# A decoder layer in split fp32: one-row conditioning vector, reordered transposes, weight remainders on GpSimd, shifted weight tiles

## The chip, the cores and the metric

One core of one Trainium2 chip runs the whole layer in one launch. The metric is device microseconds. The kernel before was timed three times: median 1067.24 us, lowest 1066.86, highest 1069.26.

## The reference, cut to what matters

The input x is 512 tokens by 1024 features, fp32. Three sub-layers follow each other; each normalises x (RMSNorm), scales and shifts it by values made from a conditioning vector c (1024 values), computes, and adds the result back to x times a gate.

```
c_act = silu(c);  mod = c_act @ w_ada + b_ada          # 9 x 1024 scales, shifts, gates
1: h = modulate(rms_norm(x));  x += 0.5 * gate * (silu(h @ Wg) * (h @ Wu)) @ Wout      # D_FF 2816
2: h = modulate(rms_norm(x));  split h @ w_in into u_pool, q_lat, kv_lat, k_rope, g_pool, g_mla
   br_pool = windowed means of u_pool, grouped product, projection
   q, k, v from rms_norm(q_lat), rms_norm(kv_lat);  8 heads of causal softmax attention -> br_mla
   x += gate * (sigmoid(g_pool) * br_pool + sigmoid(g_mla) * br_mla) @ w_out
3: as 1, with its own weights
```

## The kernel before, in words

**Arithmetic.** Every large product is made of three matmuls in a reduced fp32 format: each operand is split into a high part (a rounded copy) and a low part (operand minus high part), and `product` (lines 456 to 461) adds high*high, low*high and high*low. Weights arrive by DMA in slots of 128 x 2048 fp32 (`w_raw[0]`, `w_raw[1]`); ScalarE (ACT) writes the high part to `w_hi`, VectorE (DVE) subtracts to get `w_lo` (`split`, line 1340), and TensorE (PE) uses both. The same is done for the activations `h_hi`, `h_lo`. Order between the engines is written out by hand: five in-order queues (PE, ACT, DVE, GpSimd or POOL, and SP for all DMAs), joined by counting semaphores. Nothing is planned at run time, so what stands behind a waiting instruction on its queue waits as well.

**Start (`first_up`, `first_modulated`).** SP issues the constants, c copied to 128 rows (`c_wide`, 512 KB), four tiles of x, then 16 tiles of w_ada and three weight chunks in turn. ACT applies silu to `c_wide` (line 1286), loads its table for square roots and squares three x tiles; DVE makes the row scales. For each of 8 feature tiles k, DVE reduces one tile of w_ada for the scale and one for the shift, PE transposes x (`turned`, line 514), ACT writes `h_hi` and the full `scaled` copy, and DVE writes `h_lo` (`first_low`, line 1537). `part(c, k)` on PE waits for `h_lo` of tile k before any of its six matmuls.

**From FFN 1 to the mixer (`norm_mix`, `mixer`).** The last output tile of FFN 1 is done by column halves (`down_last`), so that the norm of tokens 0 to 255 (half 0) starts early. Half 0's norm runs on DVE as `scale_pair`, `low_pair` (pairs of tiles), with ACT's `high` between; the weight chunks LAT 0 and LAT 1 (2016 columns each) are split among them: ACT `mix_first(0)`, `mix_first(1)`, `mix_split(1)`, DVE the same three. PE runs half 0's latent products for k = 0..7, with `norm_sum(1, 1)` (sums of squares of half 1, needs ACT's `last_square(1, 1, ...)`) after k = 1 and `norm_wide(1, 1)` (spreads the scales of half 1, needs DVE's `norm_diag`) after k = 7. Later PE computes four pool groups, then turns the latents (line 728), then starts the KV products, which wait for all four pool groups to be copied out of PSUM (`u_evac` 4).

**Keys and heads.** PE turns 8 query heads, computes gate unit 0 (24 x 2 matmuls of 8 k), turns 8 key heads (line 790) and starts head 0. ACT takes `k_hi`, DVE `k_lo` (line 1777) per head; DVE then runs `gate(0)` (line 1770), and the row maxima, scales and splits of head 0. The probabilities are transposed by PE at line 840 once `p_scaled` counts four.

**Merge and output product.** For tile m of 8, DVE gates `tanh_mla` (line 1845), POOL adds `br_pool` (line 2038), ACT takes the high part, DVE the low part (line 1590). In the midst of it, at m = 4, ACT and DVE split the first chunk of w_out. The last chunk of w_out and the first two chunks of FFN 2 are done by column halves, beside the norm of sub-layer 3 (`norm_ffn2`, `up_by_halves`).

The lines that say where a wait stands:

```
def part(c, k):
    pe.wait_ge(h_ready, k + 1)
...
    pe.wait_ge(u_evac, 4)                      # ahead of the KV products
...
    pe.wait_ge(k_t_evac, 5)                    # ahead of head 0
```

Of the kernel before, what the change touches and what calls it, by code (L numbers as in the profile page):

```python
# [5 lines left out]
ALU = mybir.AluOpType  # L6
# [58 lines left out]
K_BANK = (1, 2, 3, 4, 0, 5, 6, 7)  # L65
# [11 lines left out]
def program(nc, x_t, x_rows, c_rows, w_ada, w_ffn_in, w_ffn_out, w_mix, mix_consts, positions, consts, out):  # L77
    ctx = ExitStack()
    with ctx:
# [22 lines left out]
        w_raw = [place(f"w_raw{i}", [P, SLOT]) for i in range(2)]  # L102
        w_hi = [place(f"w_hi{i}", [P, SLOT], F32R) for i in range(2)]
        w_lo = [place(f"w_lo{i}", [P, SLOT], F32R) for i in range(2)]
        const_sb = place("const_sb", [P, P + 72 + 3 * KD])
# [25 lines left out]
        c_wide = place("c_wide", [P, D], at=scaled_at + 4096)  # L131

# [8 lines left out]
        w0_lo = place("w0_lo", [P, SLOT], F32R, at=w0_at + 8 * SLOT)  # L141
        first_raw, first_w_hi, first_w_lo = (w0_raw, w_raw[1], w_raw[0]), (w0_hi, w_hi[1], w_hi[0]), (w0_lo, w_lo[1], w_lo[0])
# [68 lines left out]
        c_in = sem("c_in")  # L211
        x_in = [sem(f"x_in{t}") for t in range(TOK)]
# [14 lines left out]
        half_lo_done = sem("half_lo_done")  # L227
        rstd_ready = sem("rstd_ready")
# [109 lines left out]
        def _(sp):  # L338
# [116 lines left out]
        def _(pe):  # L455
# [7 lines left out]
            def w_tile(slot, t):  # L463
                cols = slice(t * P, (t + 1) * P)
                return w_hi[slot][:, cols], w_lo[slot][:, cols]

# [23 lines left out]
            def ffn(f):  # L490
# [26 lines left out]

                def part(c, k):
# [13 lines left out]
                def first_up():  # L532
# [3 lines left out]
                    part(0, 0)  # L536
# [38 lines left out]
                def up_half(s, hf, k):  # L575
                    hi, lo = ((w_hi[0], w_lo[0]), (w0_hi, w0_lo))[s]
# [6 lines left out]
                def up_by_halves():  # L583
# [3 lines left out]
                    for k in range(KD):  # L587
                        pe.wait_ge(half_ready[0], KD + k + 1)
                        up_half(0, 0, k)
                        if k == 2:  # L590
                            norm_sum(2, 1)
                        if k == 7:
                            norm_wide(2, 1)
                    pe.wait_ge(spare_lo, 1)
                    pe.wait_ge(gu_evac, NF + 2)
                    for k in range(KD):
                        up_half(1, 0, k)
# [15 lines left out]
                def down_last():  # L613

                    pe.wait_ge(out_evac, KD)
                    for hf in range(2):
                        for half in range(2):
                            pe.wait_ge(lo_done, n0 + NF + 14 + half + 1)
                            for k in range(NFH):
                                cols = half_cols(hf)  # L620
                                last = product(bank[5 + hf][:, cols], w_tile(half, k),
# [47 lines left out]
            def mixer():  # L669
# [11 lines left out]
                for k in range(KD):  # L681
                    if k < 3:
                        pe.wait_ge(half_lo_done, 2)
                    elif k < 6:
                        chunk(LAT_AT)
                    else:
                        chunk(LAT_AT + 1)
# [5 lines left out]
                    if k == 7:  # L693
# [1419 lines left out]
```

## Time and profile before

| what | value |
|---|---|
| median of 3 runs | 1067.24 us (1066.86 to 1069.26) |
| the profiled execution's own time, and its span | 1066.83 us, 1065.0 us |
| PE busy (matmul) | 1037.0 us, 97% |
| PE weight loads | 877.5 us, 82% |
| DVE, ACT, POOL busy | 537.1, 374.3, 62.0 us |
| DMA | 138.64 MB, mean 130 GB/s; 36% of the 16 engines |
| chain that ended last, share of PE | 93% |

PE's busy time counts overlapping matmuls once, and says little of its rate: what counts is from one start to the next. A 512-column matmul starts every 0.227 us in the long stages, a 256-column one every 0.12 us. The span is cut at the instructions; 1.83 us of the run's time lie around it. Times of rows are microseconds from the start of the span; "x2" on a row means two instructions merged.

### The profile page before, as it was taken

The numbers are of one execution on the slowest core, as the hardware profiler recorded it, in microseconds if no ns is written. First come the engines' busy times: TensorE is split into PE (matmuls) and PEld (weight loads), VectorE is DVE, ScalarE is ACT, GpSimd is POOL, SyncE is SP. The second block draws the span as 40 slices with busy tenths as digits, with TensorE's granted clock in tenths as the row PEclk, the third lists the DMA queues.
The fourth block names the chain that finished last, engine by engine and source line by source line (L and its number), as shares of the span: only waits on it lengthen the run. The fifth ranks groups of instructions, "written<-read, shape, count | busy, mean of one in ns | idle before, by whom it ended". The sixth has DMA issues, their size and how long they took to land.

```text
span 1065.0 us, 12725 instructions
## 1 busy us (share of the span) xinstructions
PE 1037.0 (97%) x4990; PEld 877.5 (82%) x4990; DVE 537.1 (50%) x754; ACT 374.3 (35%) x522; POOL 62.0 (6%) x56
## 2 busy tenths in 40 slices
PE   2999999999999999999999999999999999999998
PEld 2888888888888899898888887898888888888887
DVE  5765656555664265777675555564333333232221
ACT  6633232232321234577544533333323223221211
POOL 0000000000000000820100003200000000000000
PEclk9999999999999999999999999999999999999999
DMA  9765454545564332223121122213222222223222
GB/s 352 298 237 202 177 217 163 228 160 200 205 236 150 115 113 93 82 80 114 45 79 50 70 79 88 93 59 114 84 95 102 83 114 79 94 81 103 88 91 96
DMA packets 28879, 138.64 MB, mean 130 GB/s; under 512 B 3248, under 2 KB 3504, under 8 KB 21168
## 3 DMA queue, kind: packets, MB, share of 16 engines
q1 hardware_dynamic: 28848, 138.23, 35.8%
q8 instruction: 19, 0.31, 0.1%
q14 instruction: 12, 0.10, 0.0%
HBM read 136.12 MB, written 2.10 MB: 130 GB/s over the span
## 4 chain that ended last, share of the span: by engine, by line
PE 93%; DVE 2%; ACT 1%; DMA 1%; issue 1%; POOL 1%; SPq 1%; DVEq 0%; ACTq 0%; POOLq 0%
PE bank L459 31%; PE bank L461 30%; PE bank L460 30%; DMA ada_first<-w_ada 1%; PE bank L840 1%; POOL h L2038 1%; ACT w_hi L929 0%; PE bank L790 0%; DVE k_lo L1777 0%; DVE tanh_mla L1845 0%; PE bank L514 0%; ACT h_hi L958 0%; DVE h_lo L1417 0%; SPq L412 0%; PE bank L479 0%
## 5 line engine op out<-in xcount | busy, mean ns | idle before, releaser
L459 PE MATMUL bank<-h_hi,w_hi 128*128 128x512 f32 (+1 forms) x976 | 373.4, 383 | 5.1 <-DVE h_lo L1537 2.8
L461 PE MATMUL bank<-h_lo,w_hi 128*128 128x512 f32 (+1 forms) x976 | 370.8, 380 | 0.0
L460 PE MATMUL bank<-h_hi,w_lo 128*128 128x512 f32 (+1 forms) x976 | 370.8, 380 | 0.0
L1342 DVE TENSOR_TENSOR w_lo<-w_raw,w_hi 128x2048 fp32r<-128x2048 f32 (+3 forms) x93 | 189.8, 2041 | 147.5 <-ACT w_hi L929 147.5
L459 PEld LDWEIGHTS bank<-h_hi,w_hi 128*128 128x128 f32 x976 | 184.4, 189 | 40.6 <-DVE h_lo L1537 3.2
L461 PEld LDWEIGHTS bank<-h_lo,w_hi 128*128 128x128 f32 x976 | 184.2, 189 | 35.1
L460 PEld LDWEIGHTS bank<-h_hi,w_lo 128*128 128x128 f32 x976 | 184.5, 189 | 33.9
L929 ACT ACTIVATE w_hi<-w_raw 128x2048 fp32r<-128x2048 f32 (+3 forms) x93 | 158.7, 1707 | 121.2 <-PE bank L461 77.8
L459 PE MATMUL bank<-act_hi,w_hi 128*128 128x512 f32 (+1 forms) x374 | 141.1, 377 | 0.0
L460 PE MATMUL bank<-act_hi,w_lo 128*128 128x512 f32 (+1 forms) x374 | 140.8, 377 | 0.0
L461 PE MATMUL bank<-act_lo,w_hi 128*128 128x512 f32 (+1 forms) x374 | 140.8, 376 | 0.0
L1220 ACT ACTIVATE scaled<-bank 128x512 f32<-128x512 f32 x44 | 26.3, 597 | 275.0 <-PE bank L461 275.0
L1875 DVE TENSOR_TENSOR scaled<-scaled,bank 128x512 f32<-128x512 f32 x44 | 30.2, 687 | 166.1 <-ACT scaled L1220 166.0
L460 PEld LDWEIGHTS bank<-act_hi,w_lo 128*128 128x128 f32 x374 | 70.4, 188 | 13.0
L461 PEld LDWEIGHTS bank<-act_lo,w_hi 128*128 128x128 f32 x374 | 70.4, 188 | 13.0
L459 PEld LDWEIGHTS bank<-act_hi,w_hi 128*128 128x128 f32 x374 | 70.4, 188 | 12.7
L1347 DVE CUSTOM_DVE_ANT_0 ada_raw<-ada_raw,c_wide,const_sb 128x1024 f32<-128x1024 f32 x56 | 69.9, 1281 | 5.1 <-DMA ada_raw<-w_ada 5.0
L1879 DVE TENSOR_TENSOR act_lo<-scaled,act_hi 128x512 fp32r<-128x512 f32 (+1 forms) x44 | 30.5, 692 | 35.6 <-ACT act_hi L1224 35.6
L1943 DVE SCALAR_TENSOR_TENSOR x<-bank,out_gate,x 128x512 f32<-128x512 f32 (+1 forms) x15 | 11.3, 751 | 61.0 <-PE bank L461 61.0
L1224 ACT ACTIVATE act_hi<-scaled 128x512 f32 (+1 forms) x44 | 27.8, 632 | 39.1 <-DVE scaled L1875 39.1
L938 ACT ACTIVATE scaled<-x 128x512 f32<-128x512 f32 (+1 forms) x13 | 8.2, 630 | 60.1 <-DVE x L1943 43.2
L1810 DVE TENSOR_TENSOR p_lo<-bank,p_hi 128x512 fp32r<-128x512 f32 (+1 forms) x24 | 13.0, 596 | 22.6 <-ACT p_hi L1007 22.6
(196 smaller groups left out, 887.3 us busy)
## 6 DMA issues: line engine op xcount, KB each, us to landing
w_raw<-w_ffn_in SPq DMA_DIRECT2D x41, 1024.0 KB, 4.8
ada_raw<-w_ada SPq DMA_DIRECT2D x56, 512.0 KB, 5.2
w_raw<-w_ffn_out SPq DMA_DIRECT2D x32, 704.0 KB, 4.0
w_raw<-w_mix SPq DMA_DIRECT2D x19, 1024.0 KB, 4.8
ada_first<-w_ada SPq DMA_DIRECT2D x16, 512.0 KB, 12.7
w_raw<-w_ffn_in SPq DMA_DIRECT2D x6, 512.0 KB, 12.8
x_tok<-x_rows SPq DMA_DIRECT2D x4, 512.0 KB, 7.2
x<-x_t SPq DMA_DIRECT2D x4, 512.0 KB, 5.6
```

The costliest lines, as they stand in the source:

```text
L459: nc.tensor.matmul(dst, a_hi, b_hi, start=start, stop=False)
L460: nc.tensor.matmul(dst, a_lo, b_hi, start=False, stop=False)
L461: return nc.tensor.matmul(dst, a_hi, b_lo, start=False, stop=stop)
L929: nc.scalar.activation(w_hi[slot][:, 0:size], w_raw[slot][:, 0:size], ACT.Copy).then_inc(hi_done, 1)
L1220: nc.scalar.activation(silu_g, bank[banks[0]][:, :], ACT.Silu).then_inc(silu_done, 1)
L1224: nc.scalar.activation(act_hi[f][:, bass.ds(j, 1), :], prod, ACT.Copy).then_inc(act_hi_done, 1)
L1342: nc.vector.tensor_tensor(w_lo[slot][:, 0:size], w_raw[slot][:, 0:size], w_hi[slot][:, 0:size].bitcast(F32), ALU.subtract).then_inc(lo_don ...
L1347: nc.vector.tensor_tensor_reduce(out=raw, in0=raw, in1=c_wide[:, :], scale=1.0, scalar=bias_ada[:, col:col + 1], op0=ALU.mult, op1=ALU.add ...
L1810: nc.vector.tensor_tensor(p_lo[:, at:at + n, :].rearrange("p b q -> p (b q)"), bank[b][:, 0:n * P], p_hi[:, at:at + n, :].bitcast(F32).rea ...
L1875: nc.vector.tensor_tensor(prod, silu_g, bank[banks[1]][:, :], ALU.mult).then_inc(gu_evac, 1)
L1879: nc.vector.tensor_tensor(act_lo[f][:, bass.ds(j, 1), :], prod.unsqueeze(1), act_hi[f][:, bass.ds(j, 1), :].bitcast(F32), ALU.subtract)\
L1943: nc.vector.scalar_tensor_tensor(out=xm, in0=bank[4 + s // 2][:, :].unsqueeze(1), scalar=out_gate[:, bass.ds(m, 1)], in1=xm, op0=ALU.mult, ...
```

## The change

1. **c as one row.** c is loaded as 1 x 1024 ahead of the constants; PE spreads it over 128 rows by two fp32 matmuls with a row of ones, ACT applies silu in two halves out of PSUM. `part_high_first(0, 0)`: the first part does its four matmuls with `h_hi` as soon as `h_hi` is there. DVE's `first_low(0)` goes ahead of `scale_tile(1)`.
2. **Norm of the mixer, remainders on GpSimd.** The low parts of LAT 0 and LAT 1 are made by POOL in four pieces of 1008 columns; ACT's high parts are in four pieces, in another order; `norm_wide(1, 1)` stands after k = 4 instead of 7, `norm_var` and `norm_diag` ahead of the last `low_pair`.
3. **Latents** are turned ahead of the last pool group.
4. **Keys.** Gate unit 0 is cut in two; four key heads are turned ahead of its second half, four after it, with new banks; head 0 waits for 4 key heads instead of 5. The low part of gate chunk 1 (2048 columns) is made by POOL; ACT's split and `gate(0)` stand after four key heads.
5. **Merge.** ACT splits the chunk of w_out at m = 2, DVE after the gating of m = 3. `gain_cols(2)` is moved out of `norm_ffn2` to ahead of the merge.
6. **Norm of FFN 2.** The first two chunks are computed together for k = 0..3, with `norm_sum` after k = 0 and `norm_wide` after k = 3; `norm_var`, `norm_diag` and ACT's `norm_std` stand earlier.
7. **64 bytes.** The split weights used by 256-column products of the last output tiles and of FFN 2's first two chunks lie 64 bytes further (`late_hi`, `late_lo`, `spare_w_hi`, `spare_w_lo`).

```diff
-K_BANK = (1, 2, 3, 4, 0, 5, 6, 7)
+K_BANK = (1, 2, 3, 0, 5, 6, 7, 4)
...
+            sp.dma_start(c_row[:, :], c_rows).then_inc(c_in, 16)
             sp.dma_start(const_sb[:, :], consts).then_inc(const_in, 16)
-            sp.dma_start(c_wide[:, :], c_rows).then_inc(c_in, 16)
...
+                def part_high_first(c, k):
+                    pe.wait_ge(first_h, 2 * k + 1)
+                    pe.wait_ge(first_lo[c], k + 1)
...                                            # hi*hi and lo*hi of both gu
+                    pe.wait_ge(h_ready, k + 1)
...                                            # hi*lo of both gu
                     else:
-                        chunk(LAT_AT + 1)
+                        pe.wait_ge(second_lo_done, 1)
...
-                    if k == 7:
+                    if k == 4:
                         norm_wide(1, 1)
+                chunk(LAT_AT + 1)
...
                     for g in range(2):
+                        if c and g:
+                            lat_turned()
...
-                unit(0, slot)
+                unit(0, slot, 0, 4)
                 pe.wait_ge(qk_tok_ready, 2)
                 for h in range(HEADS):
+                    if h == 4:
+                        unit(0, slot, 4, KD)
...
-                pe.wait_ge(k_t_evac, 5)
+                pe.wait_ge(k_t_evac, 4)
...
             def norm_mix():                    # ACT
                 last_square(1, 0, 7, 1)
                 norm_std(1, 0)
                 mix_first(0)
+                high(1, 0, 0)
+                high(1, 0, 1)
                 mix_first(1)
+                high(1, 0, 2)
+                high(1, 0, 3)
+                mix_second(0)
+                last_square(1, 1, 7, KD + 2)
+                high(1, 0, 4)
+                high(1, 0, 5)
+                norm_std(1, 1)
+                mix_second(1)
...
                 query_high(0)
-                mix_split(GATE_AT + 1)
-                gate(0)
                 for h in range(HEADS):
+                    if h == 4:
+                        mix_split(GATE_AT + 1)
+                        gate(0)
...
                 for m in range(KD):            # ACT, merge
-                    if m == 4:
+                    if m == 2:
                         mix_split(WOUT_AT)
...
                 for m in range(KD):            # DVE, merge
-                    if m == 4:
-                        mix_split(WOUT_AT)
...
+                    if m == 3:
+                        mix_split(WOUT_AT)
...
+            def chunk_low(k, cols):            # POOL
+                slot = (MIX_CHUNK + k) % 2
+                pool.wait_ge(hi_done, MIX_CHUNK + k + 1)
+                return nc.gpsimd.tensor_tensor(w_lo[slot][:, cols], w_raw[slot][:, cols], w_hi[slot][:, cols].bitcast(F32),
+                                               ALU.subtract)
...
             pool.wait_ge(qk_t_ready, 2 * HEADS)
...                                            # mask_wide, two small instructions
+            chunk_low(GATE_AT + 1, slice(0, SLOT)).then_inc(lo_done, 1)
```

## Rows read from the trace of the kernel before

**Rows 1.** What PE waited for: us in total, times, longest.
```profile
PE bank L459 <- DVE h_lo L1537: 2.8, 1, 2.8
PE bank L459 <- DVE h_lo L1590: 1.9, 1, 1.9
PE bank L459 <- DVE k_lo L1777: 1.5, 1, 1.5
PE bank L479 <- ACT sq_last L949: 0.8, 1, 0.8
```

**Rows 2.** Timeline of the start: start, us, engine, line, operation, tiles.
```profile
8.93 1.06 ACT L1291 ACTIVATE square_note<-x_tok 128x1024 f32<-128x1024 f32 x1 [1.04 <-DMA x_tok<-x_rows]
17.93 0.78 ACT L1210 ACTIVATE h_hi<-bank,mod,gain_mod 128x512 fp32r<-128x512 f32 x1
...
20.48 0.69 DVE L1537 TENSOR_TENSOR h_lo<-scaled,h_hi 128x512 fp32r<-128x512 f32 x1
```

**Rows 3.** DMA issues: KB each, median us from issue to landing.
```profile
const_sb<-consts SPq DMA_DIRECT2D x1, 112.0 KB, 2.1
```

**Rows 4.** Timeline around an fp32 matmul of 256 columns (L487), PE.
```profile
382.29 0.59 PE L487 MATMUL bank<-diag,ones_r 128*128 128x256 f32 x2
382.53 0.47 PE L459 MATMUL bank<-act_hi,w_hi 128*128 128x256 f32 x1
382.83 0.28 PE L460 MATMUL bank<-act_hi,w_lo 128*128 128x256 f32 x1
```

**Rows 5.** Timeline of the mixer's norm, DVE.
```profile
383.71 1.20 DVE L1432 TENSOR_TENSOR w_lo<-w_raw,w_hi 128x1008 fp32r<-128x1008 f32 x1
385.03 0.89 DVE L1417 SCALAR_TENSOR_TENSOR h_lo<-scaled,mod,h_hi 128x256 fp32r<-128x256 f32 x2
```

**Rows 6.** Timeline, POOL: a 16-column and a 512-column subtraction or addition.
```profile
448.01 0.22 POOL L2017 TENSOR_TENSOR window<-window,mixc 128x16 f32<-128x16 f32 x1
...
341.69 1.30 POOL L1986 TENSOR_TENSOR ssq<-ssq,scaled 128x512 f32<-128x512 f32 x1 [13.60 <-ACT scaled L938]
```

**Rows 7.** Timeline, DVE beside POOL, two places.
```profile
640.60 1.30 POOL L2038 TENSOR_TENSOR h<-tanh_mla,br_pool 128x512 f32<-128x512 f32 x1
641.33 1.12 DVE L1590 TENSOR_TENSOR h_lo<-h,h_hi 128x512 fp32r<-128x512 f32 x1 [1.27 <-ACT h_hi L1007]
...
445.54 1.49 DVE L1342 TENSOR_TENSOR w_lo<-w_raw,w_hi 128x1152 fp32r<-128x1152 f32 x1
445.89 2.04 POOL L2014 TENSOR_TENSOR window<-window 128x512 f32<-128x512 f32 x1
446.95 1.12 DVE L1590 TENSOR_TENSOR lat<-lat,mixc 128x128 f32<-128x128 f32 x1
```

**Rows 8.** Timeline of the latents' end, ACT and PE.
```profile
440.97 0.60 ACT L1007 ACTIVATE u_pad<-bank 128x512 f32<-128x512 f32 x1 [4.84 <-PE bank L461]
...
443.73 0.47 PE L459 MATMUL bank<-w_hi,lat_hi 128*128 128x512 f32 x1 [0.62 <-DVE lat_lo L1663]
```

**Rows 9.** Timeline of head 0's start, DVE and PE.
```profile
507.49 0.68 DVE L1770 SCALAR_TENSOR_TENSOR br_pool<-scaled,br_pool 128x512 f32<-128x512 f32 x1
...
511.05 1.27 DVE L1803 TENSOR_SCALAR p_tok<-p_tok,row_inv 128x128 f32<-128x128 f32 x4
...
513.42 1.25 PE L840 MATMUL bank<-const_sb,p_tok 128*128 128x128 f32 x10
```

**Rows 10.** Timeline after the merge, PE; and its window (third last column: granted clock).
```profile
655.12 0.50 PE L459 MATMUL bank<-h_hi,w_hi 128*128 128x512 f32 x1 [1.87 <-DVE h_lo L1590]
656.55 0.63 PE L460 MATMUL bank<-h_hi,w_lo 128*128 128x512 f32 x1
656.98 0.63 PE L461 MATMUL bank<-h_lo,w_hi 128*128 128x512 f32 x1
...
655.12:662.00 6.88, 6.88 (x23) 5.36 (x24) 3.65 (x3) 3.83 (x5) 0.00 (x0) 0.75 0.04 6
```

**Rows 11.** Timeline of the last norm, DVE.
```profile
689.17 1.26 DVE L1401 SCALAR_TENSOR_TENSOR gain_mod<-mod,const_sb 128x8 f32<-128x8 f32 x1
```

More of the change, by code:

```diff
@@ L516, in turned @@
                     last.then_inc(x_turned, 1)
+                def part_high_first(c, k):
+                    cols = [slice((gu * KD + k) * P, (gu * KD + k + 1) * P) for gu in range(2)]
+                    pe.wait_ge(first_h, 2 * k + 1)
+                    pe.wait_ge(first_lo[c], k + 1)
+                    for gu in range(2):
+                        dst = bank[first_banks[c][gu]][:, :]
+                        nc.tensor.matmul(dst, first_w_hi[c][:, cols[gu]], h_hi[:, k, :], start=True, stop=False)
+                        nc.tensor.matmul(dst, first_w_lo[c][:, cols[gu]], h_hi[:, k, :], start=False, stop=False)
+                    pe.wait_ge(h_ready, k + 1)
+                    for gu in range(2):
+                        nc.tensor.matmul(bank[first_banks[c][gu]][:, :], first_w_hi[c][:, cols[gu]], h_lo[:, k, :],
+                                         start=False, stop=False)
                 def part(c, k):
@@ L620, in down_last @@
                                 cols = half_cols(hf)
-                                last = product(bank[5 + hf][:, cols], w_tile(half, k),
+                                last = product(bank[5 + hf][:, cols], late_tile(half, k),
                                                (act_hi[0][:, half * NFH + k, cols], act_lo[0][:, half * NFH + k, cols]),
@@ L913, in mixer @@
                             last.then_inc(tail_done, 1)
+            pe.wait_ge(c_in, 16)
+            pe.wait_ge(one_row_ready, 1)
+            for half in range(2):
+                nc.tensor.matmul(bank[half][:, :], one_row[:, :], c_row[:, S * half:S * half + S], start=True, stop=True)\
+                    .then_inc(c_spread, 1)
             pe.wait_ge(const_in, 16)
@@ L967, in mix_first, with mix_second @@
                     .then_inc(hi_done if part else half_hi_done, 1)
+            def mix_second(part):
+                act.wait_ge(raw_in[1], 16 * ((MIX_CHUNK + 1) // 2 + 1 - RAW_LATER[1]))
+                act.wait_ge(pe_used, FFN_CHUNKS)
+                n = MIX_SIZES[1] // 2
+                nc.scalar.activation(w_hi[1][:, n * part:n * part + n], w_raw[1][:, n * part:n * part + n], ACT.Copy)\
+                    .then_inc(hi_done if part else second_hi_done, 1)
             def norm_mix():
@@ L1266, in down @@
                         if not (last and s == 3):
-                            split((n0 + NF + s + 1) // 2 + 2 * i, (s + 1) % 2, OUT_ELEMS, (pe_used, u0 + q), f)
+                            split((n0 + NF + s + 1) // 2 + 2 * i, (s + 1) % 2, OUT_ELEMS, (pe_used, u0 + q), f,
+                                  late_hi if f == 0 and last and s else w_hi)
                         elif after:
@@ L1282, in ffn @@
                 down(3, True)
-            act.wait_ge(c_in, 16)
-            nc.scalar.activation(c_wide[:, :], c_wide[:, :], ACT.Silu).then_inc(c_ready, 1)
+            for half in range(2):
+                act.wait_ge(c_spread, half + 1)
+                nc.scalar.activation(c_wide[:, S * half:S * half + S], bank[half][:, :], ACT.Silu).then_inc(c_ready, 1)
             act.wait_ge(const_in, 16)
@@ L1929, in down @@
                         if not (last and s == 3):
-                            split(n0 + q + 1, (s + 1) % 2, OUT_ELEMS)
+                            late = f == 0 and last and s
+                            split(n0 + q + 1, (s + 1) % 2, OUT_ELEMS, late_hi if late else w_hi, late_lo if late else w_lo)
                         elif after:
```

152 lines of the change are left out of this document (87 added, 65 removed).

## Prediction

> **What bounds the kernel now.** I read the waits of TensorE (PE) first, then the timeline around each of them. PE is busy 97% of the span, so only its stops and its rate count. The reader is to see in [rows 1] how small the stops are: outside the start, 2.8 us before the first product of FFN 1, 1.9 us in the output product, 1.5 us ahead of head 0, 0.8 us in the mixer's norm; there are four more of 0.3 to 0.6 us. In the timelines one looks for the last event before each stop. At the start it is `h_lo` of tile 0 [rows 2]: `h_hi` is complete at 17.93 + 0.78 = 18.71, `h_lo` ends at 21.17, PE begins at 21.23. In the output product it is the low part of merged tile 6, and the stop costs more than 1.9 us: after it the matmuls start 0.43 us apart (656.55, 656.98) where 0.227 is the pace, and the window's granted clock is 0.75 [rows 10]: TensorE ran part of it at 1.2 GHz. Everything else on DVE, ACT and the queues has slack as long as it does not reach one of these places.
>
> I walked each stage through its queues in order, with the durations of the rows. The walk of the old order gives 396.1 for the second `norm_wide` (trace 396.3) and 655.2 for the product after the stop (trace 655.12), so the same walk of the new order is worth something. All sums are made against the profiled execution, 1066.83 us, which lies 0.4 us under the median.
>
> **A, the start.** `c_wide` (512 KB) leaves the queue, so x lands up to 1.3 us sooner. ACT does not gain all of it. The row of c lands about 2.1 us after its issue at 0.73, as `const_sb` did [rows 3]: 2.85. The price of the spreading: an fp32 matmul of 256 columns moves PE's next start by 382.83 - 382.29 - 0.12 = 0.42 us [rows 4], four passes over the columns at 2.4 GHz. So 512 columns at 1.2 GHz take 4 x 512 / 1.2 = 1.71 us, and two of them end at 6.3; silu's second half 7.0; the table of 1.3 us and a warm-up 8.5. The squares that began at 8.93 [rows 2] begin at 8.5, and -0.45 us is what reaches the row scales. PE then need not wait for `h_lo`: it starts at 18.71 - 0.45 + what ACT's order costs, about 18.8 instead of 21.2, does four products at the slow pace, and finds `h_lo` of tile 0 made (19.5 to 20.2, one w_ada reduction of 1.2 us sooner). Then the cover is gone: the next tiles' `h_lo` become the bound, since DVE's row of reductions is only 0.1 to 0.5 us ahead, and PE waits 0.24 us for tile 1 and 0.4 us for tile 2. The walk ends `first_up` 2.0 us sooner. Bounds: 1.5 (the row of c lands 0.5 later) and 2.8 (the spreading at full clock). **A = -2.0.**
>
> **B, the mixer's norm.** Before, DVE made the low parts of LAT 0 and 1 in 1.12 + 1.12 + 2.17 us; now POOL does, in four pieces of 1008 columns. Its price is not in the trace; from 0.22 us for 16 columns and 1.30 for 512 [rows 6] it is 0.22 + 992 x 2.18 ns = 2.38 us (bounds: 2.05, by the additions of 1.04 us, and 2.56, by proportion from 1.30), against 1.20 on DVE [rows 5]. What decides is that the two engines do not run side by side. At 641.33 DVE's `h_lo` of 512 columns took 1.12 us instead of 0.69 [rows 2], and ended 0.55 us after POOL's addition of 640.60 to 641.90 [rows 7]: it stood still until 0.13 us before POOL's end. At 445.89 it was POOL that stood still behind DVE's `w_lo`, and when that ended POOL went first, though DVE's next was issued too: that one took 1.12 us for 128 columns. All DVE instructions that waited this way read two SBUF operands. `low` (L1417) does, and so do the small steps of `norm_diag`. So each `low` can wait for a whole piece of 2.38 us. The walk: the first piece 383.6 to 386.0; PE starts k = 0 on time at 386.67; `low` of tile 0 at 385.85, then POOL's second piece 386.25 to 388.6 holds `low` of tile 1, so k = 1 starts at 389.0 instead of 387.6; tile 2 and all of ACT behind its `high(1, 0, 2)`, `mix_second(0)` and the square follow, and `norm_sum` starts at 391.8 (before: 389.5); the third piece (391.3) holds `low` of tile 4, the fourth (395.9 to 398.2) holds `norm_diag`, and `norm_wide` runs at 398.8 with k = 5, 6, 7 still to do. Half 1 begins at 405.7; before, at 400.2. **B = +5.45**, bounds +3.5 (2.05 us, pieces of 1.9 even) and +6.1. If POOL and DVE did not hold each other, it would be -1.1: the 0.8 us wait of [rows 1] goes, since the square is done when PE asks, and the rest is overlap.
>
> A rule speaks to just this. The Trainium skill, "SBUF — State Buffer", "Who interferes with whom", says that a VectorE instruction with two SBUF inputs and a GpSimd instruction that reads SBUF take the same read port, and that the one that came second waits out the other. The trace agrees, 1.12 us against 0.69. It gives B = +5.45 where a plain count of freed DVE time would give -1.1. The same skill, "GPSIMD Engine Reference", "Performance versus the Vector engine", has 4497 ns for a fp32 addition of 2048 columns on GpSimd; my line through the rows gives 4.65; with the page's figure B and D would be 0.3 us smaller.
>
> **C, latents.** The transposes (2.1 us) move ahead of the last pool group. The stop at 443.73 [rows 8] was for the low part of the latents; that one is made beside the group now. But `u_evac` 4 stands in the same place: the copy of the last group began 0.2 us after PE's end and took 0.6 (440.97 [rows 8]). It is late next: the stop of 0.9 us from start to start comes back as 0.8. **C = 0**, bounds -0.1 and +0.2.
>
> **D, keys and head 0.** Four key heads are turned before the second half of the unit, so their `k_lo` (0.66 each) is made beside it: PE can start head 0 at 504.0 instead of 505.94. ACT, behind its split and `gate(0)`, has `k_hi` 7 at 505.6, DVE its `k_lo` at 506.35. But POOL begins the subtraction of 2048 columns, 0.22 + 2032 x 2.18 ns = 4.65 us, after the mask, at 504.8, and holds the port until 509.3. DVE's `gate(0)` reads `scaled` and `br_pool`, both in SBUF, and stands still from 506.35 to 509.3; behind it on DVE stand the row maxima and `p_scaled`. Before, `gate(0)` at 507.49 led to the last `p_scaled` at 511.05 + 1.27 = 512.32, so 4.83 us later [rows 9]; now 509.3 + 4.83 = 514.15. PE's transposes, at 513.42 before without a wait, start at 514.2, and PE has stood 2.8 us. **D = +0.8**, bounds -1.9 (nothing held; the 1.5 of [rows 1] gone) and +1.2.
>
> **E, merge and output product.** With the split at m = 2 ACT does it (1.9 us) in its pause for POOL, and DVE's subtraction lies after tile 3 instead of 644.41. The walk has `merged_low` 6 at 652.9 instead of 655.1 and `merged_low` 7 at 653.8: PE wants them at 653.1 and 653.8, and stops 0.1 us. That is 2.1 us of stop, and with it goes the slow stretch: from 655.96 to 659.4 eight starts came 0.43 apart or nearly, 1.6 us lost [rows 10]. **E = -3.7**, bounds -2.0 (the slow stretch comes anyway) and -3.8. `gain_cols(2)` has 24 us of room where it now is.
>
> **F, the last norm.** `gain_cols(2)` took 1.26 us on the path, since it too stood behind POOL (689.17 [rows 11]). Without it the half outputs start with PE's end, 0.5 us sooner, and `norm_sum` waits 0.3 instead of 0.8; the second stop (0.6 us) keeps 0.35, as the sum now stands after k = 0 and ACT's square is late there. **F = -0.75**, bounds -0.3 and -1.2.
>
> **G, 64 bytes.** 420 matmuls of 256 columns are touched, at 0.12 us from start to start; the columns alone are 0.107. Ends: -5.6 us (all 13 ns gone) and +4.2 (10 ns more, the spread of the 336-column tiles, whose offsets alternate by 64 bytes: 0.148 to 0.164). Their mean is the same for both offsets, so I take **0**.
>
> **Sum.** -2.0 + 5.45 + 0 + 0.8 - 3.7 - 0.75 + 0 = -0.2. A stop of 1.9 us was followed by the slow clock at 655, one of 1.5 us at 505.94 was not [rows 1, 10]. B now stops PE 1.4, 1.8 and 3.3 us within 11 us: I add the price of one slow stretch, +1.6, for it, and none for D, whose stop stands alone. +1.4 on 1066.83 is **1068.2 us**; this case's own range is 1065 to 1071.
>
> **The rivals.** *1: the port doesn't bind.* If pieces of 1008 columns let DVE in between, or DVE goes first, B = -1.1 and D = -1.9: -2.0 - 1.1 - 1.9 - 3.7 - 0.75 = -9.4, 1057.4 us. For it: 1008 columns aren't in the trace, and DVE loses 4.4 us of work in a tight place. Against: [rows 7] and all other meetings of the two. *2, slower: D's stop drops the clock as well.* Place: PE after 514.2; price 1.6 us [rows 10]; it decides if 2.8 us of standing is enough, where 1.9 us was. 1069.8 us. For it: the length; against: PE worked without a pause before it. *3: the 64 bytes pay.* 7 ns of 13 over 420 matmuls, -2.9: 1065.3 us. For it: the 336-column tiles do react to offsets; against: their mean.
>
> **How the numbers follow.** What can be told from no change is 0.2%, 2.1 us: 1065.1 to 1069.4. Chances: forecast 0.50 (faster 0.08, same 0.30, slower 0.12), rival 1 0.27 (faster), rival 2 0.15 (same 0.03, slower 0.12), rival 3 0.08 (faster 0.05, same 0.03). Together faster 0.40, same 0.36, slower 0.24. The range of 8 in 10 reaches from the middle of rival 1, 1056.5, to the upper bounds of B with a slow stretch, 1071.5.
>
> **What would show it.** A: first product near 18.8, `first_up` over 2 us sooner. B: `h_lo` (L1417's successor) at up to 2.4 us while POOL subtracts, POOL pieces near 2.4 us, stops of PE between 387 and 399 (in old times). D: `gate(0)` of near 3.6 us on DVE and a stop of 2.8 us before the transposes of head 0. E: no stop over 0.3 us in the output product and granted clock 1.00 there. G: 0.12 us between 256-column starts. Wrong it would be if `low` kept its 0.48 us beside POOL, or if the 256-column pace moved.

## The result, and the profile after

The changed kernel takes 1082.25 us (median of 4 runs, 1080.15 to 1083.08) against 1067.15 us (1066.86 to 1069.26): ratio 1.0135, 95% interval [1.0122, 1.0149]. It is slower by 15 us, where I had 1068.2 and a range up to 1071.5. The profiled execution took 1081.75 us, with a span of 1079.9. Of all the runs reported below one, of the kernel of experiment 9, took 3796.43 us and counts in no ratio.

The page of the kernel after, its span and the head of its first part:

```profile
span 1079.9 us, 12740 instructions
...
PE 1058.1 (98%) x4994; PEld 886.1 (82%) x4994; DVE 541.1 (50%) x751; ACT 374.8 (35%) x524; POOL 78.9 (7%) x61
```

PE is even busier than before, so its rate is the place to look. Two windows of 100 us in the long stages, FFN 1 and FFN 2; columns: window, length, busy time (instructions) of PE, weight loads, DVE, ACT, POOL, then granted clock, DMA share, GB/s. The kernel before:

```profile
200.00:300.00 100.00, 100.00 (x442) 82.78 (x442) 56.97 (x69) 28.26 (x29) 1.91 (x2) 1.00 0.55 197
740.00:840.00 100.00, 100.00 (x443) 82.78 (x442) 34.57 (x28) 27.32 (x27) 0.00 (x0) 1.00 0.26 94
```

The kernel after:

```profile
200.00:300.00 100.00, 100.00 (x434) 81.96 (x433) 55.15 (x67) 28.15 (x29) 1.71 (x2) 1.00 0.56 197
740.00:840.00 100.00, 100.00 (x435) 81.90 (x434) 33.06 (x27) 27.33 (x27) 0.00 (x0) 1.00 0.27 95
```

No stop in either, the granted clock is 1.00 in both, and yet 8 matmuls fewer in 100 us. No edit of the change reorders the work of these loops. The timeline of PE shows which matmuls are late (start, duration), first before, then after:

```profile
200.50 0.39 PE L459 MATMUL bank<-h_hi,w_hi 128*128 128x512 f32 x1
200.73 0.39 PE L460 MATMUL bank<-h_hi,w_lo 128*128 128x512 f32 x1
200.95 0.39 PE L461 MATMUL bank<-h_lo,w_hi 128*128 128x512 f32 x1
201.18 0.39 PE L459 MATMUL bank<-h_hi,w_hi 128*128 128x512 f32 x1
```

```profile
200.67 0.40 PE L471 MATMUL bank<-h_hi,w_hi 128*128 128x512 f32 x1
200.90 0.40 PE L472 MATMUL bank<-h_hi,w_lo 128*128 128x512 f32 x1
201.14 0.39 PE L473 MATMUL bank<-h_lo,w_hi 128*128 128x512 f32 x1
201.36 0.40 PE L471 MATMUL bank<-h_hi,w_hi 128*128 128x512 f32 x1
```

Before, three products take 0.68 us from start to start; after, 0.69. Over 240 triples between 100 and 350 us the means of the three are 232.5, 234.1 and 226.7 ns after; before they were 226.6, 226.4 and 227.0 ns. The slow ones are the starts on either side of the product with the low weights; from the third product to the next first one nothing changed. Outside the stops and after 50 us, 3,767 matmuls of 512 columns start 231.15 ns apart on average; before it was 226.87. That is 3,767 x 4.28 = **16.1 us**, more than the whole loss. The 411 matmuls of 256 columns went the other way, from 119.86 to 113.98 ns, -2.4 us. After, in the last norm:

```profile
723.04 0.28 PE L472 MATMUL bank<-h_hi,late_lo 128*128 128x256 f32 x1
723.16 0.28 PE L473 MATMUL bank<-h_lo,late_hi 128*128 128x256 f32 x1
723.27 0.28 PE L471 MATMUL bank<-h_hi,late_hi 128*128 128x256 f32 x1
```

The rest looks as the walk had it. What PE waited for in the kernel after (us in total, times, longest); it answers to [rows 1]:

```profile
PE bank L882 <- DVE p_tok L1856: 2.6, 1, 2.6
...
PE bank L495 <- ACT sq_last L996: 2.0, 2, 1.6
PE bank L471 <- DVE h_lo L1480: 1.3, 1, 1.3
PE bank L471 <- issue: 0.7, 1, 0.7
```

The 1.9 us of the output product and the 1.5 us ahead of head 0 are gone. New are 2.6 us for `p_tok` of head 0 and two or three stops in the mixer's norm. The start, which answers to [rows 2]:

```profile
16.80 0.78 ACT L1271 ACTIVATE h_hi<-bank,mod,gain_mod 128x512 fp32r<-128x512 f32 x1
...
17.62 0.79 PE L541 MATMUL bank<-h_hi,w_hi 128*128 128x512 f32 x1 [0.57 <-ACT h_hi L1271]
...
18.27 0.69 DVE L1587 TENSOR_TENSOR h_lo<-scaled,h_hi 128x512 fp32r<-128x512 f32 x1 [1.56 <-ACT scaled L1271]
```

PE starts 0.6 us before `h_lo` is begun, as the split of the first part allows. In the mixer's norm, POOL's pieces and DVE's small steps, which answer to [rows 5, 7]:

```profile
386.68 2.38 POOL L2065 TENSOR_TENSOR w_lo<-w_raw,w_hi 128x1008 fp32r<-128x1008 f32 x1 [8.91 <-ACT w_hi L1013]
389.01 2.53 POOL L2059 TENSOR_TENSOR w_lo<-w_raw,w_hi 128x1008 fp32r<-128x1008 f32 x1
...
387.10 4.72 DVE L1480 SCALAR_TENSOR_TENSOR h_lo<-scaled,mod,h_hi 128x256 fp32r<-128x256 f32 x2 [0.30 <-ACT h_hi L1005]
...
398.52 2.32 DVE L1429 SCALAR_TENSOR_TENSOR rstd<-newton,rstd 128x2 f32<-128x2 f32 x1
```

Two `low` of 0.48 us each take 4.72 us together, and a step of two columns takes 2.32: each stood until a piece of POOL was done. The same at the keys, which answers to [rows 9], with the granted clock behind it (third last column of the window):

```profile
514.35 4.61 POOL L2059 TENSOR_TENSOR w_lo<-w_raw,w_hi 128x2048 fp32r<-128x2048 f32 x1
...
515.81 3.70 DVE L1824 SCALAR_TENSOR_TENSOR br_pool<-scaled,br_pool 128x512 f32<-128x512 f32 x1
...
523.72 1.99 PE L882 MATMUL bank<-const_sb,p_tok 128*128 128x128 f32 x10 [2.58 <-DVE p_tok L1856]
...
525.94 0.63 PE L472 MATMUL bank<-h_hi,w_lo 128*128 128x512 f32 x1
526.36 0.63 PE L473 MATMUL bank<-h_lo,w_hi 128*128 128x512 f32 x1
...
523.70:528.00 4.30, 4.28 (x17) 3.76 (x18) 2.61 (x5) 3.27 (x5) 0.00 (x0) 0.60 0.01 2
```

And at the latents, ACT's last pool copy and the KV products behind it, answering to [rows 8]:

```profile
451.36 0.60 ACT L1067 ACTIVATE u_pad<-bank 128x512 f32<-128x512 f32 x1 [4.24 <-PE bank L473]
...
452.06 0.47 PE L471 MATMUL bank<-w_hi,lat_hi 128*128 128x512 f32 x1 [0.73 <-issue]
```

### The profile page after: what moved, and what is told of

It is laid out like the page before. It is cut to its first block, busy times and chain, and to the rows that moved or that the text cites. A ratio compares the mean times of both kernels' runs of the same rounds, so it can differ in the third digit from the quotient of the medians.

```text
span 1079.9 us, 12740 instructions
## 1 busy us (share of the span) xinstructions
PE 1058.1 (98%) x4994; PEld 886.1 (82%) x4994; DVE 541.1 (50%) x751; ACT 374.8 (35%) x524; POOL 78.9 (7%) x61
## 4 chain that ended last, share of the span: by engine, by line
PE 95%; DVE 1%; ACT 1%; DMA 1%; issue 0%; SPq 0%; DVEq 0%; ACTq 0%
PE bank L471 31%; PE bank L472 31%; PE bank L473 30%; DMA w_raw<-w_ffn_in 1%; PE bank L882 1%; DVE h_lo L1480 0%; PE bank L829 0%; DVE br_pool L1824 0%; PE bank L495 0%; PE bank L530 0%; ACT k_hi L1193 0%; DVE k_lo L1830 0%; ACT h_hi L1005 0%; ACT p_tok L1201 0%; PE bank L756 0%
## 5 line engine op out<-in xcount | busy, mean ns | idle before, releaser
L471 PE MATMUL bank<-h_hi,w_hi 128*128 128x512 f32 x878 | 350.4, 399 | 0.0
L472 PE MATMUL bank<-h_hi,w_lo 128*128 128x512 f32 x878 | 349.4, 398 | 0.0
L473 PE MATMUL bank<-h_lo,w_hi 128*128 128x512 f32 x878 | 342.8, 390 | 0.0
L473 PEld LDWEIGHTS bank<-h_lo,w_hi 128*128 128x128 f32 x878 | 169.2, 193 | 38.6
L471 PEld LDWEIGHTS bank<-h_hi,w_hi 128*128 128x128 f32 x878 | 165.5, 188 | 36.9
L472 PEld LDWEIGHTS bank<-h_hi,w_lo 128*128 128x128 f32 x878 | 165.6, 189 | 33.8
L472 PE MATMUL bank<-act_hi,w_lo 128*128 128x512 f32 x330 | 131.1, 397 | 0.0
L471 PE MATMUL bank<-act_hi,w_hi 128*128 128x512 f32 x330 | 130.9, 397 | 0.0
L473 PE MATMUL bank<-act_lo,w_hi 128*128 128x512 f32 x330 | 128.6, 390 | 0.0
L1201 ACT ACTIVATE p_tok<-bank,row_max 128x128 f32<-128x128 f32 (+3 forms) x32 | 16.9, 528 | 23.1 <-DVE row_max L1846 22.4
```

The lines of the kernel that those rows point to most:

```text
L471: nc.tensor.matmul(dst, a_hi, b_hi, start=start, stop=False)
L472: nc.tensor.matmul(dst, a_lo, b_hi, start=False, stop=False)
L473: return nc.tensor.matmul(dst, a_hi, b_lo, start=False, stop=stop)
L1201: nc.scalar.activation(p_tok[:, at:at + qt + 1, :].rearrange("p b q -> p (b q)"), bank[qt][:, 0:(qt + 1) * P], ACT.Exp, bias=row_max[:, qt ...
```

## The experiments

The theory after this reading: the loss is the address of the low weights. Edit 7 needs room for the shifted tiles, and makes it with 128 bytes between `w_hi` and `w_lo` and 128 more behind `w_lo`. Before, `w_hi`, `w_lo`, `h_hi`, `h_lo` and `act_hi` all begin 128 bytes past a multiple of 512, and tiles are 512 bytes apart. After, the low weights begin 256 past one, and all that lies behind them, `act_hi` too, 384 past one. So counted modulo 256 bytes the low weights alone have left the common place. Two buffers are said to be in phase when they begin at the same place modulo 256. The rival: the new order of work puts other traffic beside the matmuls.

**1. Only the gaps.** The kernel before, and

```diff
+        cursor[0] += 128
         w_lo = [place(f"w_lo{i}", [P, SLOT], F32R) for i in range(2)]
+        cursor[0] += 128
```

> The kernel before with one edit: 128 bytes of free space between w_hi and w_lo, and 128 more behind w_lo. Nothing is reordered and nothing lies at +64. Theory 1 (addresses): the low weights lie 128 bytes off the phase of the high weights, and that alone makes the 512-column pitch 0.231 instead of 0.227 (0.2325, 0.234, 0.2267 for the three products). 3,775 such matmuls after 50 us by 4.3 ns, and 100 before: 1067.2 + 16.6 = 1083.8 us. Rival 2 (the order of the work): the pitch rose because the new order leaves other traffic beside the matmuls; then this kernel is at 1067.2 us and 0.227.

Measured 1081.75 us against 1066.66, ratio 1.0137 [1.0121, 1.0154]; 231.14 ns between 3,786 starts. Its long stages:

```profile
200.00:300.00 100.00, 100.00 (x435) 81.84 (x434) 55.81 (x70) 26.35 (x27) 0.61 (x1) 1.00 0.56 198
740.00:840.00 100.00, 100.00 (x435) 81.84 (x434) 33.05 (x27) 27.32 (x27) 0.00 (x0) 1.00 0.26 95
```

435 matmuls in 100 us, as in the changed kernel, with not one instruction moved. The rival is out: two free gaps of 128 bytes cost 15 us. The pitch alone would make it 16.2 (3,786 x 4.27 ns); about 1.6 of that is hidden because this execution has no stretch at 1.2 GHz behind the stop of the output product (granted clock 1.00 between 655 and 670), which the one of before has [rows 10]. The second gap moves everything behind the low weights by 256 bytes as well; experiment 3, in which only the tiles move, and experiment 9 show that this is not what costs.

**2. The change without edit 7.** The changed kernel; both gaps removed, and

```diff
-        late_hi = [... at=cursor[0] + 4 * SLOT * i + 64) ...]     # late_lo, spare_w_hi, spare_w_lo alike
+        late_hi = [... at=cursor[0] + 4 * SLOT * i) ...]
```

> The changed kernel without its seventh edit: no gaps, and the tiles of the 256-column products at their old addresses. Theory 1: pitches 0.227 and 0.120 again, 1082.2 - 16.6 + 2.6 = 1068.2 us; it also is the sum that I had forecast for edits 1 to 6. Rival 2: it stays near 1082 us, pitch 0.231.

Measured 1067.86 us (11 runs) against 1066.66 (15 runs): 1.0005 [0.9995, 1.0014], pitches (from one start to the next) 226.89 ns at 512 columns and 119.86 at 256. Edits 1 to 6 together change nothing that can be told. As the pitch is that of before, its trace can be laid beside the one of before stage by stage; this is used below.

**3 and 4. Which offsets.** Weights of FFN 2's down projection at offsets of their own for each chunk, products of 512 columns in one kernel, of 2 x 256 in the other:

```diff
+OFFS = [(high, low), ...]
-    last = product(bank[4 + mm][:, :], w_tile(half, k), ...)
+    oh, ol = OFFS[2 * m + half]
+    tile = (w_hi[half][:, oh + k * P:oh + k * P + P], w_lo[half][:, ol + k * P:ol + k * P + P])
```

> The kernel before; in the 16 chunks of FFN 2's down projection each chunk's high and low weights are written and read at byte offsets of their own (loops unrolled for it): (high, low) = (0,0) (64,64) (0,128) (64,192) (128,128) (192,192) (256,256) (32,32) (384,384) (0,64) (64,0) (0,256) (0,32) (448,448) (96,96) (0,512). 33 matmuls of 512 columns each. Theory 1a, only the difference high to low counts: 0.2267 for all equal pairs and (0,512), 0.231 for the others. Theory 1b, the place itself counts (all tiles start 128 bytes past a multiple of 512 in the kernel before): equal pairs differ from each other; (64,64) at 0.220, by the 7 ns that the 256-column products gained. Rival 2: 0.227 everywhere.

> As the map of 512 columns, but each product of FFN 2's down projection is done in two column halves of 256, each in its own PSUM bank, with the same 16 pairs of offsets; twice the matmuls, so some 1067 + 7 us. Theory 1a: 0.120 for equal pairs, and (64,192) no better than (0,128). Theory 1b: (0,0) 0.120, (64,64) and (64,192) 0.113 as in the changed kernel; the rest shows which offset pays.

Mean ns from start to start, 33 matmuls (512 columns) and 66 (256) for each pair, added to the place of before:

```
high, low   0,0   0,256 0,512 256,256  0,128 128,128 64,192 0,64  64,0  64,64 192,192 448,448 384,384 0,32  32,32 96,96
512 cols   226.6 227.0 226.8 227.3    231.5 232.5   231.9  231.1 233.0 233.4 229.1   229.2   232.0   233.2 233.0 234.2
256 cols   119.9 120.0 119.8 120.0    119.3 118.6   113.7  117.7 117.8 117.8 117.8   117.7   120.0   118.4 118.3 118.7
```

The border from the pair (0,0) to (64,64) in the timeline of the first of the two: starts 0.22 to 0.23 apart up to 949.29, 0.23 to 0.24 behind it.

```profile
948.84 0.39 PE L462 MATMUL bank<-act_hi,w_lo 128*128 128x512 f32 x1
949.07 0.39 PE L463 MATMUL bank<-act_lo,w_hi 128*128 128x512 f32 x1
949.29 0.40 PE L461 MATMUL bank<-act_hi,w_hi 128*128 128x512 f32 x1
949.53 0.39 PE L462 MATMUL bank<-act_hi,w_lo 128*128 128x512 f32 x1
949.76 0.40 PE L463 MATMUL bank<-act_lo,w_hi 128*128 128x512 f32 x1
```

Each of the two kernels ran once (1069.06 and 1072.47 us). Theory 1a falls: in (64,64) and (128,128) high and low weights are in phase with each other and still cost 6 to 7 ns. 1b holds as to the place, but its number does not: no pair brings 512 columns under 226.6. Pairs that are alike modulo 256 agree within 0.7 ns, with one exception: (128,128) and (384,384) at 256 columns, 118.6 and 120.0. The kernel before has the best place for 512 columns and one of the worst for 256, and the two want different ones. That the pair (0,256) is as good as (0,0) is the way out for a layout that needs room.

**5 and 6. Place against what.** (Run once each, 1072.97 and 1072.66 us.) Tiles 576 bytes apart in FFN 2's down projection, so that each chunk walks through all phases; then the same with the moving operands 64 bytes further:

```diff
+    # ACT and DVE write, PE reads: tile k at k * (P + 16) elements; low weights 16 * m elements further
 act_hi = [place(f"act_hi{f}", [P, NF, S], F32R, at=act_at) ...]        # second kernel: at=act_at + 64, act_lo alike
```

> The kernel before; in FFN 2's down projection the weight tiles lie 576 bytes apart instead of 512, so that tile k of a chunk begins 64 k bytes further than before (mod 512), and the low weights of output tile m begin 64 m bytes further still. In the first chunk of each m the matmuls have 512 columns, in the second they are done in halves of 256. This scans all 8 x 8 pairs of phases in steps of 64 bytes. If only the phase modulo 256 counts: 0.227 for 512 columns where both phases are 0 or 256, 0.229 to 0.235 elsewhere; for 256 columns 0.120 there, 0.118 elsewhere and 0.1135 where high and low are 128 apart and neither is at 0 or 128 (the map had 0.1137 at (64,192)). If the phase modulo 512 counts, (320,320) differs from (64,64), as the changed kernel's spare tiles suggest: there both halves lie at 320 and the pitch was 0.113.

> The same scan with the moving operands act_hi and act_lo 64 bytes further. Theory P, the place of the weights alone counts: the same table. Theory Q, the place of the weights against that of the moving operand counts: the whole table is shifted by one step along the diagonal, and (64,64) has the 0.227.

The row of both tables in which the low weights lie 64 bytes past the high ones, mean ns of the three products of 512 columns for tiles k = 0 to 10 (place of the high weights 64 k):

```
moving at 0:    233.7 232.7 230.0 232.3 227.3 230.0 237.0 232.3 227.0 230.3 236.7
moving at +64:  229.3 228.3 230.0 237.0 232.3 227.3 230.3 236.7 232.3 227.3 229.7
```

From k = 4 on the second row is the first shifted by one tile: what counts is where the weights lie against the moving operand, theory Q. Over all eight rows, k = 5 to 9, the second kernel's tiles differ from the first's by 0.5 ns on average when shifted by one tile and by 2.8 when not, and those of 256 columns by 0.1 and 1.6. The shift fails in one kind of row, at 512 columns where high and low weights are in phase with each other; there it misses by up to 2.7 ns. The pattern comes back after four tiles, 256 bytes, from k = 3 on in the row shown (its first three do not fit it), and rows whose low weights differ by 256 bytes agree within 0.7 ns from k = 1 on. Not all of the expectation came: two tiles in phase with the moving operand take 230.7 to 231.0 in the first kernel and 230.3 to 232.7 in the second, never 227 but for the very first tile (226.7), and the (64,192) of 256 columns is not at 113.5 but at 118 here. In these kernels a tile's neighbours lie elsewhere too; that this makes the difference is likely and not shown, so the tables with constant offsets are the ones to use.

**7 and 8. Edits 2 and 4 undone; edit 2's order with DVE.** Both without edit 7; the second keeps the new order of the norm and puts the four remainders back on DVE (`mix_low`, between the pairs):

```diff
                 scale_pair(1, 0, 0)
+                mix_low(0, 0, half_hi_done, 2, half_lo_done)
                 low_pair(1, 0, 0)
+                mix_low(0, 1, hi_done, MIX_CHUNK + 1, lo_done)
                 scale_pair(1, 0, 2)
```

> The changed kernel without edits 2, 4 and 7: mixer norm and keys as before, the start, the latents, the merge and the last norm as changed. Theory (the stages add up as the trace of the kernel without edit 7 shows them): -2.15 start, +0.1 latents, -3.7 merge, -0.5 last norm: 1066.7 - 6.2 = 1060.5 us. Rival: the merge was only in time because the stops before it had let DVE and ACT run ahead; then the output product stops again and it is 1063 to 1064 us.

> As the one without edits 2, 4 and 7, but with edit 2's new order of the mixer norm, its four remainders of 1008 columns made by DVE instead of GpSimd. Theory (the shared port costs, not the order): no stop over 0.8 us between 384 and 400, and 0.5 to 1.5 us faster than the kernel without edit 2: 1059.3 us. Rival (the new order itself costs the 4.9 us of the mixer norm): 1065.3 us.

Measured 1060.27 us, ratio 0.9921 [0.9901, 0.9941], and 1061.85, 0.9938 [0.9916, 0.9959]; the kernel before had its median at 1069.14 in the runs beside these (7, from 1066.34 to 1070.21), against 1066.66 and 1067.21 beside the other experiments, so these two ratios flatter by some 0.2%. The first is the sum of the stages to 0.2 us. The second did not bring its 1.2 us, nor did the new order cost 4.9: in its trace the stage of the norm costs 1.4 us more than in the first's, and most of that is a stretch at 1.2 GHz behind a stop of 1.4 us. Its window:

```profile
384.00:400.00 16.00, 14.93 (x89) 14.63 (x88) 14.58 (x37) 8.61 (x18) 0.37 (x3) 0.89 0.36 123
```

(1.00 in the same window of the first.) So at least 3.4 of the 4.9 us are the GpSimd remainders', and the new order without them gains nothing. The port shows directly: with no piece of POOL beside it, the step of two columns that took 2.32 us takes 0.16, and two `low` take 0.87 us instead of 4.72.

The first's trace has such a stretch elsewhere. The keys are untouched in it, and yet behind the same stop of 1.5 us:

```profile
505.60 0.63 PE L469 MATMUL bank<-h_hi,w_hi 128*128 128x512 f32 x1
506.03 0.63 PE L470 MATMUL bank<-h_hi,w_lo 128*128 128x512 f32 x1
506.46 0.63 PE L471 MATMUL bank<-h_lo,w_hi 128*128 128x512 f32 x1
...
503.00:512.00 9.00, 8.45 (x34) 7.04 (x35) 6.38 (x20) 3.43 (x11) 3.48 (x4) 0.81 0.10 41
```

while the kernel before, at the same place, has

```profile
505.90:515.00 9.10, 9.06 (x49) 7.85 (x50) 6.14 (x20) 4.31 (x13) 2.97 (x4) 1.00 0.04 16
```

The same code after the same stop ran at 1.2 GHz for a while in one execution and not in the other: 1.6 us. The profiled execution of the first kernel took 1061.85 us, its other three, at a mean granted clock of 1.000 instead of 0.998, 1060.05 to 1060.33.

**9. The change with its layout mended.** The changed kernel, with

```diff
-        cursor[0] += 128
-        late_lo = [... at=cursor[0] + 4 * SLOT * i + 64) ...]
+        cursor[0] += 256
+        late_lo = [... at=cursor[0] + 4 * SLOT * i + 192) ...]
```

and 256 bytes behind `w_lo` instead of 128.

> The changed kernel with one edit: the two gaps are 256 bytes instead of 128, and the shifted low weights lie at +192 instead of +64. So w_lo is back in phase with w_hi and with the moving operands, while the 256-column products keep the pair (64,192), which the map had at 0.1137. Theory (relative place modulo 256 bytes): 512 columns 0.2267, 256 columns 0.1135, all else as changed: 1082.2 - 16.6 = 1065.5 us. Rival (any gap costs, or 256 is not the period in all slots): 1069 to 1082 us.

Measured 1066.01 us, 0.9983 [0.9971, 0.9995] against before (1067.21, 17 runs); 226.89 and 113.73 ns, and 443 matmuls in the window again:

```profile
200.00:300.00 100.00, 100.00 (x443) 82.82 (x442) 58.30 (x71) 27.11 (x28) 1.91 (x2) 1.00 0.56 191
```

Its three numbers, 256, 192 and 256, are worth 16.2 us. In this trace the shifted tiles bring 0.7 us in FFN 1's last output tile and 1.5 us in the last norm over the kernel without edit 7.

**10 and 11. The versions that the runs point to.** Edits 1, 3, 5, 6 and the mended 7; then also edit 4's order, with the remainder of the gate chunk on DVE:

```diff
                 query_low(0)
-                mix_split(GATE_AT + 1)
                 for h in range(HEADS):
+                    if h == 4:
+                        mix_split(GATE_AT + 1)
                     dve.wait_ge(k_hi_done, h + 1)
```

> Edits 1, 3, 5 and 6 with the mended layout; the mixer norm and the keys as before (no remainders on GpSimd). 1060.3 - 2.6 = 1057.7 us. If the 256-column pitch was hidden behind waits in the halves (the norm bound, not PE), under 1.5 us is gained and it is above 1058.8 us.

> As the last, with edit 4's order of keys and gate unit 0, but the remainder of gate chunk 1 made by DVE after the fourth key head, not by GpSimd. Theory (the port, not the order, cost the 2.8 us of that stage): head 0 starts 1.7 us sooner, PE then meets p_scaled at about 512.3 in old times and keeps 1.1 us: 1056.6 us. Rival (DVE is late by its own work there): at 1057.7 us or above.

Measured 1059.57 us, 0.9928 [0.9914, 0.9943], and 1057.45 us, 0.9911 [0.9897, 0.9925]. The first's six runs lie at 1058.1 to 1058.2 (two) and 1059.4 to 1060.3 (four), and the median is over my bound of 1058.8; the profiled one is of the lower group, at 1058.13, and in its trace the 256-column stages bring 2.1 us over those of the kernel without them. A slow stretch of 1.6 us, as above, would make the two groups, and the mean granted clock agrees: 1.000 in both runs of the lower group and 0.998 in all four of the upper one. No trace of the upper group was taken, so where it lies is open. Of the second's six runs four lie at 1057.3 to 1057.5 (clock 1.000) and two at 1058.7 and 1059.1 (0.998). In its trace head 0 starts 1.67 us sooner, and 0.7 of that is kept when PE asks for `p_scaled`; I had expected 1.1 and 1056.6 us:

```profile
PE bank L881 <- DVE p_tok L1863: 0.8, 1, 0.8
```

The intervals of the two overlap, but runs of the same granted clock do not: at 1.000 the second takes 1057.29 to 1057.49 us and the first 1058.13 and 1058.19, 0.75 more, as the traces say. So the order of edit 4 gains 0.7 us, and what it cost in the changed kernel came with the GpSimd remainder.

**12. The pair (64,64) instead of (64,192).**

```diff
-        late_lo = [... at=cursor[0] + 4 * SLOT * i + 192) ...]
+        late_lo = [... at=cursor[0] + 4 * SLOT * i + 64) ...]
```

> As the kernel with the keys' remainder on DVE, but the shifted low weights lie at +64, not +192, so high and low are in phase: pair (64,64). The map of 256 columns had 0.1178 there and 0.1137 at (64,192); in the map each tile is used for both halves in turn, here once. In the changed kernel the spare tiles had (64,64) too, and 0.113. If the map carries over: 308 matmuls of the shifted slots at 0.1178, +1.3 us, 1058.7 us. If the spare tiles carry over, the pair (64,64) is as good: 0.113 and 1057.4 us, and the gap of 128 bytes was never needed for the 256-column products.

Measured 1058.86 us, 0.991 [0.9893, 0.9928] (before: 1067.05). The 316 matmuls of the shifted slots are at 116.0 ns, between the 117.8 of the map and the 113.9 of (64,192); the 95 of the spare tiles at 114.2. So the 128 bytes between high and low do pay for 256 columns, about 0.7 us in all. The rest of the 1.4 us is not the pair's: this trace begins FFN 1 at 18.60, that of experiment 11 at 17.82. Why the spare tiles, also at (64,64), do not need the 128 bytes is open; modulo 512 they are at (64,64) and the shifted ones at (64,320).

## Why the prediction was wrong

**G, 64 bytes: the step that failed.** I took it at 0, between -5.6 and +4.2, for "420 matmuls of 256 columns are touched". Measured: -2.4 us on these (rival 3's mechanism, at 5.9 of 13 ns instead of 7), and +16.1 us on 3,767 matmuls of 512 columns that I had not counted at all. With the +1.5 of edits 1 to 6 below, 1066.83 + 1.5 - 2.4 + 16.1 = 1082.0, and the profiled execution took 1081.75. The error is in the question "what does the edit touch". The diff line `cursor[0] += 128` moves every buffer placed behind it, `w_lo` among them, which one of three products reads and the one before it stands next to. I had the hint in my own text: "the 336-column tiles, whose offsets alternate by 64 bytes: 0.148 to 0.164" suggests that a place changes a matmul's pace. I used it for the 420 that the edit names, and not for the 3,800 that it moves.

The Trainium skill, "TensorE: Matmul & The Clock Gate", "Step-by-step: what each phase is for", says that loading the next tile's weights takes no read bandwidth from the running matmul. By that one would not expect the place of the weights to matter. Here the mean pace changes from 226.6 ns to 229 to 234 with nothing but the place of the weights against the moving operand, and the measurement decides; whether the load or something else makes it, no run shows.

**Edits 1 to 6.** I had -0.2 + 1.6 = +1.4 us on 1066.83. The trace of the kernel without edit 7 has +1.5 at its last matmul, and the comparison 1.0005 [0.9995, 1.0014]. By stages, from the starts of the first matmuls behind each (us, before and without edit 7):

```
                                   before   without 7   stage    forecast
first product of FFN 1              21.23    18.23                 18.8
FFN 1 down                         265.10   262.95     -2.15   A  -2.0
pool groups begin (behind B)       418.97   421.70     +4.88   B  +5.45, and +1.6 clock
KV products                        443.73   446.58     +0.12   C   0
head 1's scores                    521.84   527.50     +2.81   D  +0.8 (rival 2: +2.4)
output product, its 256 columns    685.54   687.52     -3.68   E  -3.7
FFN 2 down                         941.76   943.22     -0.52   F  -0.75
```

**A** and **E** are right in place and size. In A the first product came earlier than the walk had it (18.23 for 18.8), and the tiles behind it gave 0.85 us back instead of 0.4. In E the stop and the slow stretch went together, as I had it; with the stretch 1.6 of the 3.7. **C** is right: PE stands 0.73 us. The view gives no releaser ("issue"), but the last pool copy ended at 451.96 in the kernel after and PE began at 452.06, so it is `u_evac` 4.

**B** has the mechanism: POOL's pieces take 2.32 to 2.53 us (forecast 2.38), `low` and `norm_diag`'s steps stand behind them. The first two stops came at 1.5 and 1.9 from start to start (forecast 1.4 and 1.8), and the fourth piece and `norm_wide` within 0.5 us of the walk (396.19, which is 398.34 in old times; forecast 398.8). The slow stretch came too (granted clock 0.91 between 384 and 402), but it lay before the third stop and was swallowed by it: between 391.5 and 394.6 twelve starts are 0.28 apart instead of 0.155, PE reaches the stop 1.4 us later, and it stands 1.6 us there instead of 3.3. DVE set the moment at which it could go on. So the step that failed in B is the +1.6 added for a slow stretch: where PE waits for DVE behind it, it costs next to nothing. In the kernel after, seventeen starts are slow there, the third stop is gone, and the stage is as long to 0.1 us (+4.97 against before, here +4.88). Stops and stretch together are 4.9 against 7.05. The windows of the kernel without edit 7, and the row at the end of the third stop:

```profile
390.00:393.00 3.00, 3.00 (x18) 3.00 (x18) 2.95 (x7) 1.20 (x3) 1.34 (x1) 0.74 0.34 89
393.00:396.00 3.00, 2.02 (x8) 1.64 (x6) 2.90 (x4) 1.06 (x3) 2.55 (x4) 0.69 0.54 211
...
396.19 0.70 PE L501 MATMUL bank<-diag,ones_r 128*128 128x256 f32 x2 [1.17 <-DVE diag L1449]
```

What PE waited for there, in the kernel without edit 7:

```profile
PE bank L880 <- DVE p_tok L1854: 2.6, 1, 2.6
...
PE bank L493 <- ACT sq_last L994: 1.9, 2, 1.6
PE bank L469 <- DVE h_lo L1478: 1.2, 1, 1.2
PE bank L501 <- DVE diag L1449: 1.2, 1, 1.2
```

Rival 1, that the port would not bind, is out: each of DVE's instructions with two SBUF inputs that met a piece of POOL ended 0.02 to 0.3 us behind that piece, `gate(0)` 0.55 behind its own.

**D** also has the mechanism: POOL 4.60 us (forecast 4.65), `gate(0)` 3.67 (near 3.6), the stop 2.6 to 3.0 (2.8). The size is off by the clock: I gave its slow stretch to rival 2 with "PE worked without a pause before it" against it. It came in both traces, and made +2.8 of +0.8; nothing swallows it there, since PE stops no more behind it. **F**: -0.52 for -0.75: from start to start the first stop fell from 0.82 to 0.47 and the second from 0.68 to 0.53, where I had 0.5 and 0.25 of gain.

The sum of edits 1 to 6 came out right by luck: B was 2.2 us too dear and D 2.0 too cheap. In both the port was sized well and the price of the slow clock was not.

## What to carry to other kernels

Ask of an edit to the memory map which buffers it moves, not which it names: two free gaps of 128 bytes changed the pace of 3,800 matmuls by 2% and cost seven times what its shifted tiles won. Make room in multiples of 256 bytes (256 cost nothing here), and read the matmul's pace (matmuls in a window of 100 us) beside the stops; a busy share of 98% hides it. Work taken from DVE to GpSimd is not free when DVE's own steps read two SBUF operands: in the new order each waited for a whole piece. Smaller pieces were not tried; the best kernel here leaves them on DVE.

## What the runs showed of the hardware

- The place of a matmul's weights against its moving operand sets its pace, with a pattern that repeats after 256 bytes, but for one pair: 512 columns 226.6 to 227.3 ns where both high and low weights are in phase with the moving operand, 229 to 234 at the other constant pairs; 256 columns 120.0 in phase, 113.7 at (64,192), 117.7 to 120.0 at the others. Why is not shown.
- A stop of 1.5 us before the same code was followed by 1.2 GHz in one execution and by 2.4 GHz in another; the difference is 1.6 us. The kernel before, whose code is the same in every run, took 1065.6 to 1066.0 us in the 7 runs beside the experiments with a mean granted clock of 1.000, 1066.3 to 1067.7 in the 25 with 0.998, 1069.1 to 1069.7 in the 11 with 0.997, 1067.9 in the one with 0.996 and 1070.2 to 1070.8 in the 4 with 0.995.
- A slow stretch cost 1.6 us where PE did not wait again behind it, and next to nothing where it ran into a wait for DVE (twelve slow starts, then a stop of 1.6 us instead of 3.3).
- A GpSimd subtraction of two fp32 operands took 2.32 to 2.53 us for 1008 columns and 4.60 for 2048, against 1.20 and 2.29 on DVE, and a DVE step of two columns took 2.32 us beside one and 0.16 without.
